# State-space scan: four items' outputs issued together, sample tokens inside the blocks, the rotation's additions as identity products on TensorE

## The reference

```python
u = (xn @ w_in)                                   # 64 groups of 16 channels
bur = einsum('btgc,gpc->btgp', ug, b_re)          # 64 complex states per group
bui = einsum('btgc,gpc->btgp', ug, b_im)
xr = fr * bur - fi * bui                          # fr, fi: folded into B
xi = fr * bui + fi * bur
acr, aci, hr, hi = associative_scan(combine, (ar, ai, xr, xi), axis=1)   # h[t] = a * h[t-1] + x[t], complex
y = einsum('btgp,gcp->btgc', hr, c_re) - einsum('btgp,gcp->btgc', hi, c_im)
z = gelu(y + d_skip * u)
ga, gb = split(z @ w_glu, 2)
out = ga * sigmoid(gb)
```

## Time and profile before

| | us |
|---|---|
| median of 3 runs | 1801.26 (1800.65 to 1802.71) |
| the profiled execution's own time | 1803.06 |
| its span in the trace | 1801.3 |
| last row of the projection to u, TensorE (L469) | 572.80 |
| first B·u product (L826) | 586.18 |
| end of the last scan (L1767) | 780.20 |
| first GLU matmul (L467) | 804.42 |

### The profile page before, as it was taken

One profiled execution on the slowest core, in us unless ns is written; L12 is line 12 of the kernel. 1 busy time (PEld: TensorE's weight loads), 2 busy tenths in 40 slices (PEclk: granted clock), 3 DMA queues, 4 the chain that ended last, 5 costly groups with the idle time before them and its releaser, 6 DMA issues.

```text
span 1801.3 us, 28235 instructions
## 1 busy us (share of the span) xinstructions
PE 1653.2 (92%) x10763; PEld 1440.2 (80%) x10763; DVE 1223.7 (68%) x1859; ACT 858.7 (48%) x1514; POOL 205.6 (11%) x195
## 2 busy tenths in 40 slices
PE   6997987899987999949699999999999999999997
PEld 4774466789976677739589998989989899998996
DVE  2257444754435966574458787888878888788885
ACT  2222434243333101114357666766667666676774
POOL 3052003910000443310000000000000000000000
PEclk9997898999998555569779999999999999999999
DMA  8164442334441000006139898888978888798881
GB/s 329 62 187 133 175 170 103 132 140 154 183 178 70 1 1 1 1 1 243 45 115 343 303 336 305 318 318 312 334 296 331 308 321 331 288 337 303 325 332 61
DMA packets 48877, 370.45 MB, mean 206 GB/s; under 512 B 6274, under 2 KB 11458, under 8 KB 20706
## 3 DMA queue, kind: packets, MB, share of 16 engines
q1 hardware_dynamic: 46274, 365.53, 55.1%
q0 software_dynamic: 1024, 2.10, 0.4%
q10 hardware_dynamic: 1440, 0.96, 0.2%
HBM read 366.43 MB, written 2.14 MB: 205 GB/s over the span
## 4 chain that ended last, share of the span: by engine, by line
PE 85%; DVE 8%; ACT 3%; issue 3%; DMA 0%; SPq 0%; POOL 0%; DVEq 0%; ACTq 0%
PE ps L955 10%; PE ps L957 9%; PE ps L956 9%; PE ps L467 5%; PE ps L469 4%; PE ps L826 4%; PE ps L976 4%; PE ps L975 4%; PE ps L468 4%; PE ps L974 4%; PE ps L455 3%; PE ps L914 3%; PE ps L838 2%; DVE ring_lo L1426 2%; PE ps L932 2%
## 5 line engine op out<-in xcount | busy, mean ns | idle before, releaser
L955 PE MATMUL ps<-split 128*128 128x256 f32 x1408 | 417.5, 297 | 3.1 <-DVE ring_lo L1900 1.6
L957 PE MATMUL ps<-split 128*128 128x256 f32 x1408 | 399.4, 284 | 0.0
L1900 DVE TENSOR_TENSOR ring_lo<-ring,split 128x2048 fp32r<-128x2048 f32 x132 | 302.4, 2291 | 54.1 <-ACT split L1318 54.1
L956 PE MATMUL ps<-ring_lo,split 128*128 128x256 f32 x1056 | 299.4, 284 | 0.0
L955 PEld LDWEIGHTS ps<-split 128*128 128x128 f32 x1408 | 269.3, 191 | 15.9 <-DVE split L1887 1.8
L957 PEld LDWEIGHTS ps<-split 128*128 128x128 f32 x1408 | 269.9, 192 | 0.0
L1318 ACT CAST split<-ring 128x1024 fp32r<-128x1024 f32 x264 | 264.9, 1059 | 0.0
L1426 DVE TENSOR_TENSOR ring_lo<-ring,chunk_hi 128x1024 fp32r<-128x1024 f32 x100 | 149.2, 1495 | 166.6 <-ACT chunk_hi L1047 166.5
L1047 ACT CAST chunk_hi<-ring 128x1024 fp32r<-128x1024 f32 x100 | 104.7, 1048 | 212.2 <-PE ps L469 165.5
L956 PEld LDWEIGHTS ps<-ring_lo,split 128*128 128x128 f32 x1056 | 202.6, 192 | 3.9
L469 PE MATMUL ps<-xn_lo,chunk_hi 128*128 128x288 f32 x608 | 183.4, 302 | 0.0
(11 more groups left out here) (324 smaller groups left out, 3169.1 us busy)
## 6 DMA issues: line engine op xcount, KB each, us to landing
ring<-wmoe SPq DMA_DIRECT2D x132, 1536.0 KB, 8.1
arena<-wmoe SPq DMA_DIRECT2D x44, 1536.0 KB, 7.8
ring<-wpre SPq DMA_DIRECT2D x41, 1536.0 KB, 6.5
ring<-ckv SPq DMA_DIRECT2D x32, 256.0 KB, 3.0
arena<-ckv SPq DMA_DIRECT2D x32, 256.0 KB, 2.9
arena<-cki SPq DMA_DIRECT2D x32, 64.0 KB, 2.4
arena<-cki POOLq DMA_DIRECT2D x32, 64.0 KB, 5.4
arena<-xt SPq DMA_DIRECT2D x1, 1152.0 KB
```

Source lines behind the costliest of these rows:

```text
L955: mm(o, xg_hi[:, buf, k, :], wg_hi[:, c.i % 2, w], start=(k == 0), stop=False)
L956: mm(o, xg_hi[:, buf, k, :], lo[:, w], start=False, stop=False)
L957: m = mm(o, xg_lo[:, buf, k, :], wg_hi[:, c.i % 2, w], start=False, stop=(k == KD - 1))
L1900: V.tensor_tensor(moe_slot_lo(slot)[:, w], moe_slot(slot)[:, w], wg_hi[:, c.i % 2, :], ALU.subtract).then_inc(S["mw_lo"], 1)
```

## The change

**1. TensorE adds.** `sum_in` on DVE is gone. TensorE's new `s_sum(i)` multiplies the four 128x128 pieces of `ab` by an identity matrix (and one by its negative, the new constant `minus`) and lets PSUM accumulate; DVE's scan reads `gin` from PSUM. The pipeline is one item longer.

**2. Four outputs together.** `s_out` handles four items at once, with the term as the outer loop and the item as the inner one, so neighbouring matmuls write different 32 partitions. POOL has five result buffers in place of two.

**3. Sample tokens inside the blocks.** `s_in` of block 0 also computes the sample columns, as separate products of 32 columns (L830); in block 1 it has 128 columns only. The sample recurrence is cut into 8 pieces that stand behind the scan in DVE's iterations 34 to 41, its TensorE part `ys` stands in iteration 44, its skip term in 46. PSUM: three banks for B·u (four before), two for `gin`.

**4. Ahead and behind.** The B matrices are built between the `chunk_low` of the projection (both parts in one buffer), and the splits `z_high`/`low` of each of the 8 column blocks follow as its GELU is done.

```diff
@@ TensorE
-        pe.wait_ge(S["bd"], 1)
+        pe.wait_ge(S["bd"], 2)
...
         def s_in(i):
-            nt = L + bk * NS
-            if i >= 4:
-                pe.wait_ge(S["pin"], i - 3)
+            if i >= 3:
+                pe.wait_ge(S["pin"], i - 2)
+                pe.wait_ge(S["xs"], min(i - 2, SJ))
             for part in range(2):
-                m = mm(ps[:, i % 4, part * nt:part * nt + nt], bt[rws, part, mch, :], u[rws, mch, bk * L:bk * L + nt],
+                m = mm(ps[:, i % 3, part * L:part * L + L], bt[rws, part, mch, :], u[rws, mch, bk * L:bk * L + L],
                        start=True, stop=True)
+            if bk == 0:
+                for part in range(2):
+                    m = mm(ps[:, i % 3, 2 * L + part * NS:2 * L + (part + 1) * NS], bt[rws, part, mch, :], u[rws, mch, TP:T],
+                           start=True, stop=True)
             m.then_inc(S["bu_mm"], 1)
...
+        def s_sum(i):
+
+            pe.wait_ge(S["pin"], i + 1)
+            if i >= 2:
+                pe.wait_ge(S["gs"], i - 1)
+            ab = v(S_AB + (i % 2) * 512, 2, 2, L)
+            o = ps[:, 5 + i % 2, 0:2 * L]
+            mm(o[:, 0:L], ident, ab[:, 0, 0], start=True, stop=False)
+            mm(o[:, 0:L], ident, ab[:, 1, 1], start=False, stop=True)
+            mm(o[:, L:2 * L], ident, ab[:, 0, 1], start=True, stop=False)
+            mm(o[:, L:2 * L], const("minus"), ab[:, 1, 0], start=False, stop=True).then_inc(S["gin"], 1)
+
+        def s_out(zi):
+
+            pe.wait_ge(S["po_out"], 4 * zi + 4)
+            if zi >= 2:
+                pe.wait_ge(S["zin"], zi - 1)
+            for term, (c, which, part) in enumerate(((0, 0, 0), (2, 1, 1), (1, 0, 1), (1, 1, 0))):
+                for qd in range(4):
+                    i = 4 * zi + qd
+                    m = mm(ps[32 * qd:32 * qd + 32, 3 + zi % 2, 0:L], ct[:, c, i % SJ, :], po_v(i, which)[:, part, :],
+                           start=(term == 0), stop=(term == 3), skip_group_check=True)
+            m.then_inc(S["y_mm"], 1)
...
-        for i in range(2 * SJ + 5):
+        for i in range(2 * SJ + 2):
             if i < 2 * SJ:
                 s_in(i)
-            if i >= 5:
-                s_out(i - 5)
+            if i >= 2:
+                s_sum(i - 2)
+            if i == 44:
+                ys()
+            if i % 4 == 1 and i >= 9:
+                s_out((i - 9) // 4)
+        s_out(15)
@@ ACT
+                if zi >= 9:
+                    z_high(zi - 9)
+        z_high(7)
@@ DVE
+        link(V.memset(v(S_NB, 2048), 0.0))
...
         for c in range(C_U + 2, C_GL + 2):
             chunk_low(c)
+            if c == C_U + 2:
+                dve.wait_ge(S["s5p"], 16)
+                b_matrix(0)
+            if c == C_U + 4:
+                b_matrix(1)
...
         def rotate_in(i):
             dve.wait_ge(S["bu_mm"], i + 1)
             if i >= 2:
                 dve.wait_ge(S["gin"], i - 1)
...
         def scan(i):
-            gin, gs = v(S_G + (i % 2) * 256, 2, L), v(S_GS + (i % 2) * 256, 2, L)
+            gin, gs = ps[:, 5 + i % 2, 0:2 * L].rearrange("p (a b) -> p a b", a=2), v(S_GS + (i % 2) * 256, 2, L)
             dve.wait_ge(S["gin"], i + 1)
...
-        for i in range(2 * SJ + 2):
+        for i in range(2 * SJ + 3):
             if i < 2 * SJ:
                 rotate_in(i)
-            if 1 <= i <= 2 * SJ:
-                sum_in(i - 1)
...
-            if i >= 2:
-                scan(i - 2)
+            if i >= 3:
+                scan(i - 3)
...
+            if SJ + 2 <= i < SJ + 10:
+                sample_step((i - SJ - 2) // 2, i % 2)
...
+            if i == 46:
+                sample_z()
             if i % 4 == 1 and 9 <= i < 2 * SJ:
                 z_in((i - 9) // 4)
-
+            if i >= 54 and i % 4 == 2:
+                low(3, (i - 54) // 4, z_hi_at)
```

More of the change, by code:

```diff
@@ L143 @@
 S_AB = S_U + KD * T
[L144 to L149, removed]
+S_G = S_AB
+S_GS = S_AB + 1024
+S_Z = S_GS + 512
+S_PO = S_Z + 256
+NPO = 5
+S_NB = S_PO
+S_TA = S_PO + NPO * 512
+S_TB = S_END
+S_TZ = A_RS
+assert S_TA + 256 <= D_CS and S_NB + 2048 <= S_TA
 M_XN = A_PH
@@ L275, in po_v @@
     def po_v(i, which):
-        return v(S_PO + (i % 2) * 512 + which * 256, 2, L)
+        return v(S_PO + (i % NPO) * 512 + which * 256, 2, L)
     def sp_(i, n=1):
@@ L844, in _, with ys @@
+        def ys():
+            pe.wait_ge(S["hs"], 1)
+            for mch in range(8):
+                for w in range(2):
+                    for qd in range(4):
+                        j = 4 * mch + qd
+                        m = mm(ps[32 * qd:32 * qd + 32, 7, mch * NS:(mch + 1) * NS], ct[:, w, j, :], xs[:, w, j, :],
+                               start=(w == 0), stop=(w == 1), skip_group_check=True)
+            m.then_inc(S["ys_mm"], 1)
+        for i in range(2 * SJ + 2):
             if i < 2 * SJ:
@@ L1269, in _ @@
                 a(xn[:, mch, bk * L:(bk + 1) * L], v(S_Z, 2, L)[:, zi % 2, :], ACT.Gelu_apprx_tanh).then_inc(S["z"], 1)
-        act.wait_ge(S["zs_in"], 1)
-        a(xn[:, :, TP:T], v(S_Z, KD, NS), ACT.Gelu_apprx_tanh).then_inc(S["zs"], 1)
-        act.wait_ge(S["z"], 16)
-        act.wait_ge(S["zs"], 1)
-        input_high(z_hi_at)
+                if zi == 9:
+                    act.wait_ge(S["zs_in"], 1)
+                    a(xn[:, :, TP:T], v(S_TZ, KD, NS), ACT.Gelu_apprx_tanh).then_inc(S["zs"], 1)
+                    act.wait_ge(S["zs"], 1)
+                if zi >= 9:
+                    z_high(zi - 9)
+        z_high(7)
         for mch in range(8):
@@ L1774, in z_in, with sample_step, sample_z @@
             V.scalar_tensor_tensor(out=v(S_Z, 2, L)[:, zi % 2, :], in0=u[:, mch, bk * L:(bk + 1) * L],
-                                   scalar=param("dskip")[:, mch:mch + 1], in1=ps[:, 4 + zi % 2, 0:L],
+                                   scalar=param("dskip")[:, mch:mch + 1], in1=ps[:, 3 + zi % 2, 0:L],
                                    op0=ALU.mult, op1=ALU.add).then_inc(S["zin"], 1)
-        for i in range(2 * SJ + 2):
+        xv = xs.rearrange("p a j (b t) -> p a j b t", b=NB)
+        abr = sp_(ABR).unsqueeze(2).broadcast_to([P, SJ, NB])
+        abi = sp_(ABI).unsqueeze(2).broadcast_to([P, SJ, NB])
+        ta, tb = v(S_TA, SJ, NB), v(S_TB, SJ, NB)
+        def sample_step(t, part):
+            hr, hi = (s0[:, 0], s0[:, 1]) if t == 0 else (xv[:, 0, :, :, t - 1], xv[:, 1, :, :, t - 1])
+            V.tensor_tensor(ta, hi if part else hr, abr, ALU.mult)
+            link(V.tensor_tensor(tb, hr if part else hi, abi, ALU.mult))
+            link(V.tensor_tensor(ta, ta, tb, ALU.add if part else ALU.subtract))
+            link(V.tensor_tensor(xv[:, part, :, :, t], xv[:, part, :, :, t], ta, ALU.add))
+        def sample_z():
+            zs = v(S_TZ, KD, NS)
+            dve.wait_ge(S["ys_mm"], 1)
+            link(V.tensor_tensor(zs, u[:, :, TP:T], param("dskip").unsqueeze(2).broadcast_to([P, KD, NS]), ALU.mult))
+            V.tensor_tensor(zs, zs, ps[:, 7, 0:KD * NS].rearrange("p (a b) -> p a b", a=KD), ALU.add).then_inc(S["zs_in"], 1)
+        for i in range(2 * SJ + 3):
             if i < 2 * SJ:
                 rotate_in(i)
-            if 1 <= i <= 2 * SJ:
-                sum_in(i - 1)
-            if i - 2 == SJ:
+            if i - 3 == SJ:
                 dve.wait_ge(S["last"], SJ)
```

115 lines of the change are left out of this document (38 added, 77 removed).

## The result

The change takes 1835.99 us (median of 4 runs, 1834.35 to 1840.55) against 1801.99 for the kernel before on the same chip: a ratio of 1.0189, interval 1.0164 to 1.0214. The forecast was 1827, between 1774 and 1850. The profiled execution took 1836.11, its span is 1834.3.

The account below looks back on a forecast made before the run. TensorE's order at 1.2 GHz was taken to bound the loop. All at 1.2 GHz came 50 us slower, all at 2.4 faster; three items in ten at 2.4 gave 26 slower, 1827, range 1774 to 1850.

Parts of the forecast that it names:

- The sum: GLU start after the loop: 854.6 all at 1.2 GHz, 775.5 all at 2.4, against 804.4 before.
- Start: Ahead of the loop: `s_in(0)` at about 576.7 in place of 586.2; first scan ends at 588.7 or 583.7, against 591.1.
- The item at 0.50: Loop at 1.2 GHz: DVE's part plus `s_sum`, 3.6 us a plain item, 5.3 with outputs, 255 for all 63.
- The item at 1.00: Loop at 2.4 GHz: 2.7 us a plain item, 2.8 with outputs, 171 for all 63.
- Scan from PSUM: DVE's scan in the loop: takes the same time reading PSUM; 0.06 more each would make the loop 8 us longer.
- The sample pieces: Sample recurrence inside the loop: 3.3 us a piece, held by POOL; 17 us added at 2.4 GHz, 5 at 1.2.
- The tail: From last scan to GLU: 2.8 us at 2.4 GHz or 3.9 at 1.2, in place of 24.2.
- The clock: TensorE's clock in the loop: mixed, three items in ten at 2.4 GHz, 26 us slower; chance 0.47.
- the likeness: Clock in the loop, judged by similar stretches of the earlier trace: rises where `s_sum` and `s_out` adjoin for 3.5 us.
- Identity products against the clock: Clock in the loop: `s_sum` on 128 rows favours a rise, idle time behind each `s_sum` speaks against it.
- The chain is serial: Loop item: DVE's iteration and `s_sum` can't overlap, so the beat is their sum, 3.6 or 2.7 us.
- the rival that it isn't: Loop: TensorE's results reach DVE sooner, beat 3.7 us at 1.2 GHz, 1831 without any rise; no chance of its own.

Follow-up runs that it names:

- run 3: The change, each B·u product on all 128 rows in place of 32 (output not the reference's): 1778.43 us, ratio 0.9867.
- run 4: The kernel before, each B·u product on all 128 rows in place of 32 (output not the reference's): 1769.48 us, ratio 0.9826.
- run 6: The kernel before with the identity products alone, outputs item by item one iteration later: 1802.06 us, ratio 1.0002.
- run 9: The change with output products item by item in place of groups of four, five result buffers kept: 1778.00 us, ratio 0.9857.
- run 12: The change plus four useless 128x128 products behind `s_sum` in iterations without an output group, except 43 to 48: 1790.05 us, ratio 0.9915.
- run 2: The change with three `ab` buffers and three PSUM banks for `gin`: 1771.29 us, ratio 0.9832.
- run 8: The change with three `ab` buffers, three `gin` banks and full-row B·u products (output not the reference's): 1725.79 us, ratio 0.9576.
- run 11: The change with three `ab` buffers, three `gin` banks and block 0's sample columns in one product: 1735.76 us, ratio 0.9646.
- run 1: The change with the sums back on DVE, all else kept: 1754.85 us, ratio 0.9738.
- run 5: The kernel before with the output groups of four alone, five result buffers on POOL: 1771.16 us, ratio 0.9827.

## Why the prediction was right, point by point

**The sum.** Mixed seven to three, the sum's two ends put the GLU at 830.9 (0.7 x 854.6 + 0.3 x 775.5). It started at 842.3, 11 later: the loop took 13 more than the mix had, the start 2 less. In the total only 7 are left of it (1836 against 1829), because 4 came back behind the GLU in the experts' products, which the forecast didn't have. That part is luck.

**Start.** Right: `s_in(0)` at 576.51 (576.7 forecast), and alone it brought what the sum had. The first scan at 585.53 lies between the two forecasts, 583.7 and 588.7, since the clock fell at 579.2.
```profile
576.51 0.68 PE L826 MATMUL ps<-arena 32*128 32x128 f32 x4 [1.64 <-issue]
```
**The item at 0.50.** The mechanism was right, its size too small. 3.75 in block 1 against 3.6:
```profile
753.01 0.45 DVE L1786 TENSOR_TENSOR_SCAN arena<-arena,ps 128x128 f32<-128x128 f32 x1
...
753.61 0.77 PE L841 MATMUL ps<-arena 128*128 128x128 f32 x2 [1.45 <-DVE arena L1786]
...
755.76 0.69 DVE L1774 TENSOR_TENSOR arena<-ps,arena 128x512 f32<-128x512 f32 x1 [2.30 <-PE ps L844]
```
`s_sum` starts 0.15 after the scan's end, and the rotation 2.15 after that; together 2.30, where I had 2.05 and some 0.1 of waits. DVE's part is 1.45, as forecast. In block 0 I had hidden `s_in` behind DVE; with the sample columns it takes 1.84 (`s_sum` at 589.60 after `s_in` at 587.76) where DVE needs 1.5, so the sample columns cost 0.7 on the 1.2 of `s_in` rather than 0.5, and TensorE's order, not the chain, sets 3.85. An output item takes 5.71 or 5.02 against 5.3. The group itself is 1.94 against 2.0:
```profile
606.99 1.94 PE L854 MATMUL ps<-arena 128*32 128x128 f32 x32
607.17 0.69 DVE L1774 TENSOR_TENSOR arena<-ps,arena 128x512 f32<-128x512 f32 x1 [2.40 <-PE ps L844]
...
608.86 1.22 PE L826 MATMUL ps<-arena 32*128 32x128 f32 x4
```
By these beats 31 x 4.32 + 32 x 4.07 = 264, where I had 255.

**The item at 1.00.** 2.83 (run 3, DVE still waiting for L844) against 2.7. A group costs little there (2.99 against 2.8), since most of it lies beside the chain.

**Scan from PSUM.** 0.47 and 0.45, no dearer than from SBUF (0.48 and 0.46 in the earlier trace rows), as assumed.

**The sample pieces.** Right in kind: one operation stands until POOL is done (715.57 + 1.36 = 716.93), the piece takes 2.9, inside my bounds, below my 3.3.
```profile
715.41 0.40 DVE L1805 TENSOR_TENSOR arena<-arena 128x256 f32<-128x256 f32 x1
...
715.57 1.36 POOL L2073 TENSOR_TENSOR arena<-arena 128x512 f32<-128x512 f32 x1 [2.12 <-DVE arena L1786]
...
715.73 1.49 DVE L1806 TENSOR_TENSOR arena<-arena 128x256 f32<-128x256 f32 x1
...
717.72 0.61 DVE L1808 TENSOR_TENSOR arena<-arena 128x256 f32<-128x256 f32 x1
```
The eight intervals from the 32nd scan on take 38.0, where the plain beats (6 x 3.75 + 2 x 5.02) make 32.5: 5.5 added, the carry between the blocks among it, against 5.

**The tail.** 3.6 against 3.9. What I had not seen is a wait before it. POOL's five buffers are freed by groups, and the last group but one (835.19) comes late:
```profile
835.19 1.08 PE L854 MATMUL ps<-arena 128*32 128x128 f32 x32
836.45 3.92 POOL L2073 TENSOR_TENSOR arena<-arena 128x512 f32<-128x512 f32 x3 [3.60 <-PE ps L854]
837.80 0.48 DVE L1785 TENSOR_TENSOR_SCAN arena<-arena,ps 128x128 f32<-128x128 f32 x1 [3.36 <-issue]
...
842.29 0.61 PE L471 MATMUL ps<-z_hi,chunk_hi 128*128 128x288 f32 x1
```
The last scan stands for 3.36, since POOL hasn't read the buffer that it writes. Had POOL gone on at 834.4, when the scan before ended, its last three would have been done some 2 us sooner; that is an estimate.

**The clock.** Mixed, as forecast, and rising where I had said: six of the seven rises come within an output group or less than 1 us behind it, the seventh (835.2) as one starts. Two windows about such a rise:
```profile
623.60:627.00 3.40, 3.40 (x40) 2.69 (x39) 1.80 (x4) 0.68 (x4) 0.64 (x1) 0.50 0.00 0
627.00:630.40 3.40, 2.70 (x23) 2.46 (x22) 1.45 (x3) 0.13 (x2) 1.92 (x3) 1.00 0.00 0
```
But the clock stood at 1.00 for 30.6 of 253.1 us in seven stretches. By the beat of 2.83 those are some 11 of the 63 items, one in six (an estimate), where I had chosen three in ten. No row gave that share, so that the time came near is in part luck here too. By measured terms, all at 0.50 the loop would have taken some 264 + 5.5 + 2 = 271, 9 more than my 262; the high stretches gave back 18, where three tenths of the 73 between my two loops are 22. So the beat was mis-sized by more than the clock.

Two readings behind the likeness were rougher than the rows. TensorE was busy without a gap for 175.7 us (600.0 to 775.7), not 190; it idled for 3.45 of the loop's first 14. And the stretch of `s_out` after which the clock rose ended in a pause of 0.61 us, in which the rise (776.1) fell:
```profile
776.34 0.41 PE L838 MATMUL ps<-arena 128*32 128x128 f32 x2 [0.61 <-POOL arena L2045]
```

**Identity products against the clock.** The reason for the low clock was partly wrong. I took the idle time behind `s_sum` for what holds it down; runs 3 and 4 show 1.00 with 4 to 6 of 20 us idle, when the 32-row products have full rows. What decided was the mix of products: with all on full rows, or with more 128-row work in each item beside the 32-row ones (runs 6, 9 and 12), the clock is at 1.00; in the change, with its shorter groups and 32-row products, it is mostly at 0.50. The Trainium skill, "TensorE: Matmul & The Clock Gate", Why this matters for your kernels, says that a continuously busy TensorE gets the full clock; run 2 contradicts that for 100 us (TensorE without a gap, at 0.50) and then agrees, with the same instructions.

**The chain is serial**, as the step on the item had it; the rival that it isn't falls with run 8 (53 us at one and the same clock). At 0.50 breaking it changed nothing in block 0 of run 2, where TensorE's order sets the beat, and took 0.38 off an item in run 11, where it doesn't.

**Not settled.** What property of the products counts. Run 12 shows that more 128-row work in an item brings the rise; whether runs 3 and 4 rise by the rows themselves or by the switches that they save, no run tells. Parts 1 and 2 without 3 and 4 weren't run. Run 2 ran block 0 for 100 us without a pause at 0.50 and then rose in it, with nothing changed in the order; and its four times differ by 17 us. The moment of the rise seems to differ from one execution to the next.

## What to carry to other kernels

Judge a part by what it does to the clock of its stage too. Here neither of two edits is slower by itself (1802 and 1771 against 1801), but in the change they cost each other's gain: without the one it takes 1755, without the other 1778. With the groups the loop stays at 0.50 (runs 1 and 5), which costs nothing as long as DVE sets the beat; the identity products put TensorE back into the chain, and then it costs. There 1.2 us more TensorE work an item, useful or not, made the kernel 46 to 58 us faster. Where two engines hand two buffers to and fro, try a third early: one more `ab` and one more PSUM bank were worth 65 us here, 53 where the clock was the same. And where DVE and POOL share a loop, see that the DVE operation which starts during POOL's has an operand in PSUM, since those with both in SBUF are what stands. No run tries that as an edit by itself.

## What was not expected of the hardware

- TensorE full at 0.50 for 100 us, then 1.00, with the same instructions (run 2).
- With B·u products on 32 rows the loop stands at 0.50, or mostly, with the same number on 128 rows at 1.00 (runs 3 and 4, windows 620 to 640).
- An addition of 128 elements on DVE takes 0.28 alone, 0.99 when it starts within POOL's 1.27 us (run 1); a scan that reads PSUM keeps its 0.47 there.
- `s_out` for four items over four column groups: 32 rows of f32 in 1.94 at 0.50 and 1.08 at 1.00, as much as the eight rows of `s_sum`.
